# One program from the output projection to the end of the first expert pass, with the table of tokens made by one-hot products

## The chip, the cores and the metric

The kernel runs on one core of a Trainium2 chip. The metric is device time in microseconds (us) of one execution. Three executions of the kernel before took 1960.2, 1954.55 and 1946.48 us, a median of 1954.55. The profiled execution is a further one. All data are float32.

The engines are named as in the profile: PE (TensorE, matmuls; its weight loads are PEld), DVE (VectorE), ACT (ScalarE), POOL (GpSimd) and SP (SyncE, which here only issues DMAs).

## The reference

One layer of a hybrid decoder over 1024 prompt tokens and 64 sample tokens: T = 1088 tokens, D = 1024. The change touches what follows the RWKV and attention heads:

```python
h = h + concatenate([rw_out, rmsnorm(att)]) @ w_out            # output projection, 1024x1024
x = rmsnorm(h, norm_ffn)                                       # router: 4 group + 32 expert logits
gsel = argmax(x @ rgw + rgb)                                   # one of 4 groups
top_p, top_i = top_k(softmax(le_sel), 2)                       # two of the group's 8 experts
wts = pg_sel * top_p / sum(top_p)
y = sum over the two experts e of wts_e * ((silu(x @ wg_e) * (x @ wu_e)) @ wd_e)   # 1024->256->1024
h = h + y
h = h + sigmoid(rmsnorm(h) @ ple_gate_w) * (p @ ple_proj)
y_out = rmsnorm_final(h)
```

## The kernel before

The kernel is a row of programs. Each is a block in which the five engines run their own instruction streams and meet at the end. Ahead of each, `g.clear` makes a small block in which POOL clears that program's semaphores one by one. The order is: `project_tokens`, `lora_inputs`, `rwkv`, `attention`, then the part that matters here, `out_projection`, `route` (two blocks), `experts`, and last `finish`. Tokens are handled in TT = 9 tiles of 128 rows, of which the last has 64.

**rwkv to attention.** `rwkv`'s SP stream ends with a wait for all its projections and then issues the load of attention's first weights (`g.w3`, 1.5 MB, line 389). Attention's first matmul (L1227) waits for it.

**out_projection** (from L1537). PE first makes nine column sums for the norm of the attention half (L1600). Then each tile takes 32 matmul passes of 512 columns: 16 for the RWKV half (L1623), 16 for the attention half (L1628), into four PSUM banks; odd tiles use the other four. DVE adds the halves to `g.h` (L1588, L1592) and ACT sums the squares (L1561). PE does nothing else in this block.

**route, first block** (from L1633). SP loads ten constants (gain of the norm, router weights, masks). DVE waits for all ten, then makes the normed rows `xn` tile by tile (L1693); SP stores them to DRAM (`g.xn`); PE turns each tile (8 transposes, L1707), ACT copies it out of PSUM, PE makes the logits (16 passes of 96 columns, L1720), DVE adds the bias (L1682). SP loads the inputs of the embedding product last, and the block ends when they have landed.

**route, second block.** DVE chooses the experts with a serial chain of small operations, each followed by a drain (L1760 to L1788), then PE counts the tokens ahead of each (`rank`, L1858 to L1860), and DVE works out for both choices k the slot of every token in a table and its row in the output (L1801 to L1824, about 36 operations for each k). POOL then writes the token numbers into the DRAM table with 18 indirect DMAs (L1879, one for each k and tile) and waits for them. Beside it PE makes the embedding product `p @ ple_proj` (L1867), and SP loads the weights of experts 0, 1 and 2.

**experts** (from L1895). After the clear come a block that sets `now`, the load of the largest count into a register, and a block that clears semaphores again. `one_pass` then loads the table into `idx` (L1936), gathers 128 rows for each of 32 experts with indirect DMAs from POOL (L1948), and runs a pipeline over the experts: turn (8 transposes, L1958), DVE copy (L2026), up (64 passes of 128 columns, L1972), silu on ACT (L2014), product on DVE (L2035), down (8 passes of 512 columns, L1982), copy and store by ACT (L2000, L2003). PE's order is up(e), turn(e+1), down(e-1). SP loads expert e into one of four slots once down(e-4) is done. A last block gathers the results (18 indirect DMAs, L2071) and adds them into `g.h` (L2052). Later passes, for experts with more than 128 tokens, stand behind a branch; with these inputs the branch isn't taken.

**finish** (from L2079) loads the gate weights, turns the normed rows, multiplies and stores the output.

Of the kernel before, what the change touches and what calls it, by code (L numbers as in the profile page):

```python
# [6 lines left out]
D = 1024  # L7
KD = D // 128
S = 1024
# [209 lines left out]
def rwkv(nc, g):  # L219

    with ExitStack() as ctx:
# [107 lines left out]
        with nc.Block() as block:  # L329
            @block.sync  # L330
            def _(sp):
# [33 lines left out]
                for j in range(-1, J + 1):  # L365
# [1164 lines left out]
WR = 96  # L1530

# [5 lines left out]
def out_projection(nc, g):  # L1537

    with ExitStack() as ctx:
        sb = lambda n, s: ctx.enter_context(nc.sbuf_tensor(n, s, f32))  # L1540
        sem = g.semaphores(nc, ctx)
        bank = g.bank
        wo = g.wo
        junk = sb("ojunk", [128, D])
        rstd = sb("orstd", [128, TT])
        summed, meaned, rooted, gained, projected, added, zeroed = (
            sem("o_" + n) for n in "summed meaned rooted gained projected added zeroed".split())
        g.clear(nc)
        with nc.Block() as block:
            @block.gpsimd  # L1550
            def _(pool):
                pool.memset(g.h[64:128, TT - 1, :], 0.0).then_inc(zeroed, 1)

            @block.scalar
            def _(act):
                act.wait_ge(meaned, 1)
                act.activation(rstd[:, :], rstd[:, :], ACT.Sqrt).then_inc(rooted, 1)
                act.wait_ge(zeroed, 1)
                for t in range(TT):
                    act.wait_ge(added, t + 1)  # L1560
                    act.activation(junk[:, :], g.h[:, t, :], ACT.Square, accum_out=g.ss[:, t:t + 1])  # L1561
                    act.drain()

            @block.vector
            def _(dve):
                c = PC["attn_norm"]
                for j in range(J):
                    dve.wait_ge(g.wo_in[J + j], 16)
                    dve.tensor_scalar(wo[:, J + j, :], wo[:, J + j, :], g.prm[:, c + j:c + j + 1], None, ALU.mult).then_inc(gained, 1)
# [806 lines left out]
```

## Time and profile before

| what | value |
|---|---|
| median of three executions | 1954.55 us |
| profiled execution | 1968.97 us, span 1967.0 us |
| PE busy | 1672.5 us (85%) |
| DVE, ACT, POOL busy | 657.9, 430.0, 70.3 us |
| mean granted TensorE clock | 0.899 |
| DMA | 247.01 MB, mean 126 GB/s |

The page's slices of the span, each a fortieth (49 us):

```profile
PE   3687997998998888898989889966599999990897
PEclk8888898898898658899999989988699999995899
DMA  3033031221000004424242530044399999956211
```

Each digit is a tenth: the share of the slice in which the engine was busy, the clock granted to TensorE, and the busy share of the DMA engines. The programs touched run from about 1158 us (slice 24) to 1821 us (slice 37). The row of PE dips at slices 26 to 28, is 9 through the expert pipeline, and is 0 where the results are gathered.

### The profile page before, as it was taken

To read this page: it belongs to the slowest core of one execution; us is meant where nothing else is said; L and a number is where in the kernel's file an instruction comes from. 1 tells how busy PE (TensorE), PEld (TensorE's weight loads), DVE (VectorE), ACT (ScalarE), POOL (GpSimd) and SP (SyncE) were. 2 spreads that over 40 slices of the span, in tenths; PEclk is the share of its full clock that TensorE was granted. 3 is DMA by queue.
4 is the path that set the end of the run, shared out by engine and by line. 5 is a ranking of instruction groups with operands and counts; after the bars stand their busy time and mean duration, and the time that the engine had idled before them with its cause. 6 is when DMAs were issued, how large, how long until landed. Compare 5 with 4: busy or idle time off the path is not lost. (4 is left out here: it accounts for less than half of the span.)

```text
span 1967.0 us, 34999 instructions
## 1 busy us (share of the span) xinstructions
PE 1672.5 (85%) x15260; PEld 1173.9 (60%) x15260; DVE 657.9 (33%) x1559; ACT 430.0 (22%) x856; POOL 70.3 (4%) x76
## 2 busy tenths in 40 slices
PE   3687997998998888898989889966599999990897
PEld 2355666576577666575766654452488888870443
DVE  3125455445455231514251532235011111114333
ACT  2131321321321210413132320022011111112233
POOL 0000000000000000000000000003100000004000
PEclk8888898898898658899999989988699999995899
DMA  3033031221000004424242530044399999956211
GB/s 119 12 58 24 5 21 15 34 15 21 16 2 9 13 21 188 162 108 162 108 162 108 222 132 0 0 165 193 128 357 364 362 374 364 370 205 214 108 43 38
DMA packets 61774, 247.01 MB, mean 126 GB/s; under 512 B 13745, under 2 KB 21169, under 8 KB 51889
## 3 DMA queue, kind: packets, MB, share of 16 engines
q1 hardware_dynamic: 49232, 201.70, 30.8%
q0 software_dynamic: 7776, 26.23, 3.6%
q10 hardware_dynamic: 4608, 16.78, 2.1%
q8 instruction: 123, 2.02, 0.5%
q14 instruction: 35, 0.28, 0.0%
HBM read 210.65 MB, written 34.04 MB: 124 GB/s over the span
## 5 line engine op out<-in xcount | busy, mean ns | idle before, releaser
L415 PE MATMUL bank<-h,w 128*128 128x352 f32 (+1 forms) x576 | 200.7, 499 | 6.4 <-DVE xb L978 6.4
L415 PEld LDWEIGHTS bank<-h,w 128*128 128x128 f32 x576 | 110.5, 199 | 70.6 <-issue 8.7
L2026 DVE COPY xgT<-bank 128x512 f32<-128x512 f32 x64 | 41.2, 686 | 319.2 <-PE bank L1958 319.2
L1972 PEld LDWEIGHTS bank<-xgT,we_g 128*128 128x128 f32 x1024 | 122.0, 196 | 17.7 <-issue 14.3
L1227 PE MATMUL bank<-h,w 128*128 128x352 f32 (+1 forms) x384 | 120.7, 477 | 9.7 <-DMA w<-in_wqkv 9.7
L1972 PE MATMUL bank<-xgT,we_g 128*128 128x128 f32 x1024 | 122.5, 279 | 2.8 <-DVE xgT L2026 2.8
L1972 PE MATMUL bank<-xgT,we_u 128*128 128x128 f32 x1024 | 119.6, 275 | 0.0
L1972 PEld LDWEIGHTS bank<-xgT,we_u 128*128 128x128 f32 x1024 | 116.9, 192 | 0.0
L1982 PE MATMUL bank<-we_d,hT 128*128 128x512 f32 x256 | 115.0, 592 | 0.0
L2169 PE MATMUL bank<-wp,unT 128*128 128x512 f32 x256 | 113.3, 601 | 0.0
L1227 PEld LDWEIGHTS bank<-h,w 128*128 128x128 f32 x384 | 74.1, 194 | 54.6 <-POOL qd L1213 10.3
L2169 PEld LDWEIGHTS bank<-wp,unT 128*128 128x128 f32 x256 | 48.9, 193 | 58.8 <-issue 58.8
L1982 PEld LDWEIGHTS bank<-we_d,hT 128*128 128x128 f32 x256 | 46.3, 191 | 46.4 <-issue 46.4
L1283 PE MATMUL bank<-ident,score 128*128 128x128 f32 x288 | 46.3, 295 | 27.2 <-ACT score L1402 14.1
L1243 PEld LDWEIGHTS bank<-w,h 128*128 128x128 f32 (+1 forms) x576 | 65.3, 186 | 2.6
L1958 PE MATMUL bank<-ident,xg 128*128 128x128 f32 x256 | 34.7, 280 | 37.4 <-DMA xg<-xn_rows,idx 37.4
L1243 PE MATMUL bank<-w,h 128*128 128x128 f32 (+1 forms) x576 | 66.0, 275 | 0.0
L1283 PEld LDWEIGHTS bank<-ident,score 128*128 128x128 f32 x288 | 32.6, 147 | 51.4 <-ACT score L1402 27.8
L2000 ACT ACTIVATE yo<-bank 128x512 f32<-128x512 f32 x64 | 34.7, 594 | 123.7 <-PE bank L1982 123.7
L1430 DVE TENSOR_TENSOR eT<-bank,sin 128x352 f32<-128x352 f32 (+1 forms) x24 | 12.8, 535 | 142.3 <-PE bank L1235 140.8
L1466 DVE CUSTOM_DVE_ANT_0 score<-bank,count 128x512 f32<-128x512 f32 (+3 forms) x96 | 50.8, 555 | 27.5 <-PE bank L1272 27.5
L1623 PE MATMUL bank<-cache,rwT 128*128 128x512 f32 x128 | 59.4, 618 | 0.0
(399 smaller groups left out, 2579.0 us busy)
## 6 DMA issues: line engine op xcount, KB each, us to landing
we_g<-in_weg SPq DMA_DIRECT2D x32, 1024.0 KB, 7.2
we_u<-in_weu SPq DMA_DIRECT2D x32, 1024.0 KB, 9.9
we_d<-in_wed SPq DMA_DIRECT2D x32, 1024.0 KB, 12.7
cache<-in_kcj SPq DMA_DIRECT2D x4, 5120.0 KB, 16.0
cache<-in_vcj SPq DMA_DIRECT2D x4, 5120.0 KB, 15.0
y_rows<-yo ACTq DMA_DIRECT2D x32, 512.0 KB
w<-in_wrkv SPq DMA_DIRECT2D x12, 512.0 KB, 11.5
w<-in_wqkv SPq DMA_DIRECT2D x4, 1536.0 KB, 18.2
```

Of the source, the lines that this page charges most:

```text
L415: mm = pe.matmul(out[:, 0:w], w3[:, KIND[q], kd, :], g.uT[:, kd, a:a + w], start=(kd == 0), stop=(kd == KD - 1))
L1227: mm = pe.matmul(bank[QK[i][n]][:, 0:w], w3[:, k, i, :], g.uT[:, k, a:a + w], start=(k == 0), stop=(k == KD - 1))
L1243: mm = pe.matmul(bank[2 + n % 2][0:rows, 128 * (t - t0):128 * (t - t0) + 128], g.uT[:, k, 128 * t:128 * t + rows], w3[:, k, 2, :], start=( ...
L1283: mm = pe.transpose(bank[x % 2][:, 128 * (b - b0):128 * (b - b0) + 128], score[:, i % 2, hh, 128 * b:128 * b + 128], g.ident[:, :])
L1466: dve.tensor_tensor_reduce(out=score[:, i % 2, hh, 512 * b:512 * b + w], in0=bank[4 + 2 * hh + (b if i >= 4 else i % 2)][:, 0:w], in1=coun ...
L1623: pe.matmul(bank[b + i][:, :], g.rwT[:, k, 128 * t:128 * t + 128], wo[:, k, 512 * i:512 * i + 512], start=(k == 0), stop=(k == J - 1))
L1958: mm = pe.transpose(bank[k // 4][:, 128 * (k % 4):128 * (k % 4) + 128], v[:, k, :], g.ident[:, :])
L1972: mm = pe.matmul(bank[2 + e % 2][:, 128 * (2 * a + f):128 * (2 * a + f) + CAP], w[:, k, 128 * f:128 * f + 128], xT[e % 2][:, k, :], start= ...
L1982: mm = pe.matmul(bank[4 + 2 * (e % 2) + c][:, :], hT[e % 2][:, f, :], weights[e % NW][2][:, f, 512 * c:512 * c + 512], start=(f == 0), sto ...
L2000: last = act.activation(yo[:, e % 2, 512 * c:512 * c + 512], bank[4 + 2 * (e % 2) + c][:, :], ACT.Copy)
L2026: last = dve.tensor_copy(xT[e % 2][:, 4 * c:4 * c + 4, :].rearrange("p k q -> p (k q)"), bank[c][:, :])
L2169: mm = pe.matmul(bank[4 + 2 * (t % 2) + i][:, :], uT[:, t % 2, k, :], wp[:, k, 512 * i:512 * i + 512], start=(k == 0), stop=(k == KD - 1))
```

## The change

Five things, all in the programs named above.

1. `out_projection`, both blocks of `route` and the first pass of `experts` are one block, `feed_forward`, with one clear of 46 semaphores ahead of it. Buffers share memory by time: norm gain and router weights lie in expert slot 1, embedding inputs and masks in slot 3, `xn` and the gather buffers in attention's `g.w3`, and slot 2 in the cache tensor whose front held `w_out`.
2. PE's order is written out: project(t), turn(t-1), logit(t-2); then embedding tiles between the last turns and logits, between the choice of experts, `rank` and `find`. Each projection bank is its own semaphore count (`evicted`), and the projection uses banks 0 to 3 alone. PE waits for all eleven constants ahead of the first project(t).
3. The table isn't written to DRAM. DVE makes `place[k]` (token x position in the expert, 1 where it fits) and `tokens[k]` (one-hot of the expert times the token number), and PE multiplies them: `idx[position, expert]` = sum over tokens. Slot and row numbers (`rows(k)`) are worked out on DVE in the pipeline, at experts 1 and 2.
4. `combine` (the results of the first pass) has a clear of 6 semaphores of its own. `later_passes` has a clear of 19 and makes the DRAM table itself, behind the branch.
5. `rwkv` issues the load of attention's first weights once the last projections are made, inside the SP loop.

```diff
@@ rwkv, SP @@
                         if jn + 2 < J:
                             load_small(jn + 2)
-
-                for q in "rkv":
-                    sp.wait_ge(s[q + "_mm"], 3 * J)
-                sp.dma_start(g.w3[:, :], g.d_wqkv[0].rearrange("p k i c -> p (k i c)")).then_inc(g.qkv_in, 16)
+                    if jn == J - 1:
+
+                        for q in "rkv":
+                            sp.wait_ge(s[q + "_mm"], 3 * J)
+                        sp.dma_start(g.w3[:, :], g.d_wqkv[0].rearrange("p k i c -> p (k i c)")).then_inc(g.qkv_in, 16)
@@ feed_forward, SP @@
+                for dst, src in LOADS:
+                    if dst is i32t:
+                        sp.wait_ge(s["summed"], 1)
+                    sp.dma_start(dst, src).then_inc(s["consts"], 16)
+                sp.dma_start(pp, g.d_pproj.rearrange("(k p) n -> p k n", p=128)).then_inc(s["p_in"], 16)
+                sp.dma_start(pT, g.d_pT.rearrange("(k p) n -> p k n", p=128)).then_inc(s["p_in"], 16)
+                load_expert(sp, g, weights[0], 0, w_in[0])
                 for t in range(TT):
...
+                sp.wait_ge(s["projected"], 4 * TT)
+                load_expert(sp, g, weights[2], 2, w_in[2])
+                sp.wait_ge(s["logits"], TT)
+                load_expert(sp, g, weights[1], 1, w_in[1])
+                sp.wait_ge(s["p_done"], TT)
+                sp.wait_ge(s["idx"], 1)
+                load_expert(sp, g, weights[3], 3, w_in[3])
+                for e in range(NW, NE):
+                    sp.wait_ge(s["down"], e - NW + 1)
+                    load_expert(sp, g, weights[e % NW], e, w_in[e % NW])
@@ feed_forward, POOL @@
+                for i in range(3):
+                    pool.wait_ge(kept[i], 16 * len(range(i, TT, 3)))
+                pool.wait_ge(s["idx"], 1)
+                for e in range(NE):
+                    if e >= NX:
+                        pool.wait_ge(s["x_turned"], e - NX + 1)
+                    pool.indirect_dma_start(xg[e % NX], None, g.xn[:, :], bass.IndirectOffsetOnAxis(idx[:, e:e + 1], 0)).then_inc(xg_in[e % NX], 16)
@@ feed_forward, PE @@
+                def find():
+
+                    for k in range(2):
+                        pe.wait_ge(s["placed"], k + 1)
+                        for t in range(TT):
+                            mm = pe.matmul(bank[7][:, 0:NE], place[k][:, t, :], tokens[k][:, t, :], start=(k == 0 and t == 0), stop=(k == 1 and t == TT - 1))
+                    mm.then_inc(s["found"], 1)
...
+                mm.then_inc(s["summed"], 1)
+                pe.wait_ge(s["consts"], 16 * len(LOADS))
+                for t in range(TT):
+                    project(t)
+                    if t >= 1:
+                        turn(t - 1)
+                    if t == 2:
+                        pe.wait_ge(s["meaned"], 1)
+                    if t >= 2:
+                        logit(t - 2)
+                pe.wait_ge(s["p_in"], 32)
+                embed(0)
+                embed(1)
+                turn(TT - 1)
+                logit(TT - 2)
+                embed(2)
+                logit(TT - 1)
+                embed(3)
+                embed(4)
+                embed(5)
+                rank()
+                embed(6)
+                find()
+                embed(7)
+                embed(8)
+                gather_turn(0)
@@ feed_forward, DVE, per tile @@
+                def normed(t):
+                    x = ffn[:, t:t + 1]
+                    dve.wait_ge(s["squared"], t + 1)
+                    dve.tensor_scalar(x, g.ss[:, t:t + 1], 1.0 / D, RMS_EPS, ALU.mult, ALU.add).then_inc(s["f_meaned"], 1)
+                    dve.wait_ge(s["f_rooted"], t + 1)
+                    dve.reciprocal(x, x)
@@ feed_forward, DVE, the choice @@
+                    op(dve.tensor_tensor(oh[k][:, :, :], oh[k][:, :, :], bt(valid[:, :], NE), ALU.mult))
...
+                dve.tensor_tensor(tokens[0], oh[0][:, :, :], bt(tokv[:, :], NE), ALU.mult)
+                dve.wait_ge(s["ranked"], 1)
+                dve.tensor_tensor(tokens[1], oh[1][:, :, :], bt(tokv[:, :], NE), ALU.mult)
+                for k in range(2):
+                    op(dve.tensor_tensor(v32[:, :, :], oh[k][:, :, :], bank[4][:, 0:TT * NE].rearrange("p (t e) -> p t e", t=TT), ALU.mult))
+                    op(dve.tensor_reduce(position[:, k, :], v32[:, :, :], AX.X, ALU.add))
+                    dve.tensor_tensor(place[k], bc(iota, 128), bt(position[:, k, :], 128), ALU.is_equal).then_inc(s["placed"], 1)
+                op(dve.tensor_reduce(most, bank[5][:, 0:NE], AX.X, ALU.max))
+                dve.tensor_copy(g.most[:, :], most)
+                dve.wait_ge(s["found"], 1)
+                dve.tensor_copy(idx[:, :], bank[7][:, 0:NE]).then_inc(s["idx"], 1)
...
+                gates()
+                gather_out(0)
+                for e in range(NE):
...
+                    if e in (1, 2):
+                        rows(e - 1)
```

`gates()` holds the seven small operations that made the weights of the two experts ahead of `rank` before.

## Rows read from the trace of the kernel before

**Rows 1.** Windows of the expert pipeline: us, busy and count of each engine, clock, DMA.

```profile
core 0: us, PE busy (x) PEld busy (x) DVE busy (x) ACT busy (x) POOL busy (x), PEclk, DMA share, GB/s
1412.00:1773.00 361.00, 359.06 (x2486) 297.30 (x2484) 50.49 (x94) 46.20 (x96) 26.29 (x28) 1.00 0.89 331
```

**Rows 2.** Timeline from rwkv to attention: start us, us, engine, instruction, [idle before <-releaser].

```profile
741.36 0.20 POOL L1211 MEMSET vt<- 64x128 f32 x1 [740.90 <-POOLq L2297]
743.02 4.44 PE L1227 MATMUL bank<-h,w 128*128 128x352 f32 x7 [9.69 <-DMA w<-in_wqkv]
```

**Rows 3.** Timeline of the output projection, PE and the last DVE operation ahead of it.

```profile
1156.15 1.29 DVE L1423 TENSOR_TENSOR sqsum<-sqsum,dscore 128x1088 f32<-128x1088 f32 x1 [1.17 <-ACT dscore L1417]
1158.56 3.85 PE L1600 MATMUL bank<-ones,sqsum 128*128 128x1 f32 x18 [3.93 <-PEq L2297]
1162.34 10.15 PE L1623 MATMUL bank<-cache,rwT 128*128 128x512 f32 x16
...
1179.19 7.03 PE L1623 MATMUL bank<-cache,rwT 128*128 128x512 f32 x16
...
1261.59 7.03 PE L1623 MATMUL bank<-cache,rwT 128*128 128x512 f32 x16
```

**Rows 4.** Timeline of the router's first block.

```profile
1288.54 0.34 POOL L1676 MEMSET zeros<- 128x290 int32 x1 [129.08 <-POOLq L2297]
...
1294.98 3.67 DVE L1693 SCALAR_TENSOR_TENSOR xn<-h,rrstd,ffn_gain 128x1024 f32<-128x1024 f32 x3 [5.58 <-DMA tok<-in_tok]
...
1302.40 1.04 PE L1707 MATMUL bank<-ident,xn 128*128 128x128 f32 x8
...
1305.03 1.04 PE L1707 MATMUL bank<-ident,xn 128*128 128x128 f32 x8
```

**Rows 5.** Timeline of the choice of experts.

```profile
1327.55 0.19 DVE L1760 TENSOR_REDUCE mx<-lg 128x9 f32<-128x36 f32 x1 [4.54 <-PEq L2297]
...
1337.00 0.46 DVE L1784 TENSOR_TENSOR cnt<-cnt,valid 128x288 f32<-128x288 f32 x1
...
1340.27 0.75 PE L1858 MATMUL bank<-cnt,upper 128*128 128x288 f32 x2
...
1341.48 10.97 PE L1867 MATMUL bank<-pp,ppT 128*128 128x512 f32 x25
```

**Rows 6.** Timeline of attention and windows behind it: PE after a gap of 3.5 us.

```profile
1110.49 0.86 PE L1283 MATMUL bank<-ident,score 128*128 128x128 f32 x2 [3.53 <-ACT score L1402]
```

**Rows 7.** Window of attention, just after that gap (columns as in Rows 1).

```profile
1112.00:1114.00 2.00, 2.00 (x10) 0.80 (x8) 0.94 (x4) 0.67 (x4) 0.00 (x0) 0.50 0.95 410
```

**Rows 8.** Timeline from the scatters to the first expert.

```profile
1386.04 0.06 DVE L1921 MEMSET now<- 128x1 f32 x1 [22.75 <-PEq L2297]
1388.26 0.34 SPq L1936 DMA_DIRECT2D idx<-table  x1
...
1390.22 0.97 POOL L1948 DMA_INDIRECT xg<-xn_rows,idx  x1 [15.04 <-DMA idx<-table]
...
1398.14 1.97 PE L1958 MATMUL bank<-ident,xg 128*128 128x128 f32 x8 [37.37 <-DMA xg<-xn_rows,idx]
...
1401.49 6.63 PE L1972 MATMUL bank<-xgT,we_g 128*128 128x128 f32 x32 [1.38 <-DVE xgT L2026]
```

**Rows 9.** Timeline of the expert pipeline: DVE's copy, and PE at experts 25 apart.

```profile
1448.49 3.73 PE L1972 MATMUL bank<-xgT,we_g 128*128 128x128 f32 x32
...
1456.72 1.29 DVE L2026 COPY xgT<-bank 128x512 f32<-128x512 f32 x2 [9.86 <-PE bank L1958]
...
1735.32 3.73 PE L1972 MATMUL bank<-xgT,we_g 128*128 128x128 f32 x32
```

**Rows 10.** Timeline of the gather of the results.

```profile
1777.80 0.94 POOL L2071 DMA_INDIRECT xg<-y_rows,row_i  x1 [56.01 <-DVE row_i L2047]
...
1782.39 1.28 DVE L2052 SCALAR_TENSOR_TENSOR h<-xg,weight,h 128x1024 f32<-128x1024 f32 x1 [4.81 <-DMA xg<-y_rows,row_i]
...
1789.42 1.92 POOL L2071 DMA_INDIRECT yo<-y_rows,row_i  x1 [0.81 <-DVE h L2052]
```

More of the change, by code:

```diff
@@ L1635, in route, with feed_forward @@
+def feed_forward(nc, g):
     with ExitStack() as ctx:
@@ new lines, in feed_forward @@
+        m2 = g.spare[:, 420:420 + 2 * TT].rearrange("p (k t) -> p k t", k=2)
+        most = g.spare[:, 440:441]
+        oh = [sb(f"oh{k}", [128, TT, NE]) for k in range(2)]
+        v32 = sb("v32", [128, TT, NE])
+        i32t = g.spare[:, 444:444 + NE]
+        valid, tokv = sb("valid", [128, TT]), sb("tokv", [128, TT])
+        pad_a, position = sb("pad_a", [128, 2, TT]), sb("position", [128, 2, TT])
+        idx = g.idx = sb("idx", [128, NE], i32)
+        ple_p = g.ple_p
+        names = ("summed meaned rooted gained projected evicted added zeroed squared f_meaned f_rooted consts xnorm turned evac logits lev "
+                 "p_in shifted exped counted ranked placed found idx p_done p_out "
+                 "x_turned xev up silu h down yev stored0 stored1").split()
@@ L1745, in route, with embed_out @@
-        pg, dl = sb("pg", [128, TT]), sb("dl", [128, TT])
-        eg = sb("eg", [128, TT, G])
-        g.clear(nc)
-        with nc.Block() as block:
+                def embed_out(t):
+                    r = rows_of(t)
+                    act.wait_ge(s["p_done"], t + 1)
+                    for i in range(2):
+                        b = 2 * (t % 2)
+                        made = bank[b + i][:, :] if t < TT - 1 else bank[b][TS * i:TS * i + TS, :]
+                        last = act.activation(ple_p[0:r, t, 512 * i:512 * i + 512], made, ACT.Copy)
+                    last.then_inc(s["p_out"], 1)
@@ new lines, in _ @@
+                c = PC["attn_norm"]
+                for j in range(J):
+                    dve.wait_ge(g.wo_in[J + j], 16)
+                    dve.tensor_scalar(wo[:, J + j, :], wo[:, J + j, :], g.prm[:, c + j:c + j + 1], None, ALU.mult).then_inc(s["gained"], 1)
+                dve.wait_ge(s["summed"], 1)
+                dve.memset(rstd, 1.0)
+                dve.memset(most, 0.0)
+                dve.drain()
+                dve.tensor_scalar(rstd[:, 0:8], bank[7][:, 128:136], 1.0 / RW, RMS_EPS, ALU.mult, ALU.add)
@@ L1824, in _ @@
-                    dve.tensor_copy(g.turn[:, k, :], over[:, :]).then_inc(placed, 1)
-                    dve.drain()
-                op(dve.tensor_reduce(most[:, :], bank[1][:, 0:NE], AX.X, ALU.max))
-                dve.tensor_copy(g.most[:, :], most[:, :])
-            @block.sync
-            def _(sp):
-                for e, slot in enumerate(g.weights):
-                    load_expert(sp, g, slot, e, w_in)
-                sp.wait_ge(w_in, 48 * len(g.weights))
+                    op(dve.tensor_scalar(t1, p, float(n), None, ALU.mult))
@@ L1895, in experts, with later_passes @@
-def experts(nc, g):
-    NW, NX = 4, 3
-    AHEAD = len(g.weights)
+                pool.wait_ge(rows, 1)
+                for n in range(2 * TT):
+                    t, k = n // 2, n % 2
+                    if n >= 4:
+                        pool.wait_ge(combined, n - 3)
+                    pool.indirect_dma_start(y[n % 4][:, :], None, g.yb[:, :], bass.IndirectOffsetOnAxis(row[:, k, t:t + 1], 0)).then_inc(y_in[n % 4], 16)
+def later_passes(nc, g):
     with ExitStack() as ctx:
@@ L1935, in _ @@
                 def _(sp):
[L1936 to L1940 removed]
+                    sp.dma_start(tok[:, :], g.d_tok).then_inc(s["tok_in"], 16)
+                    sp.dma_start(g.table[:, :], g.d_zeros).then_inc(s["zero_in"], 16)
```

762 lines of the change are left out of this document (394 added, 368 removed).

## The prediction

> **What bounds the kernel now.** I read the waits of PE first, then the windows by stage, then the timeline across every border of the programs touched. PE is the bound wherever it has work: through the expert pipeline it is busy 359.06 of 361 us at the full clock [rows 1], and in the output projection it runs tile after tile with no gap [rows 3]. So time can come only from the stretches in which PE waits. The largest ends at the first expert: PE sits idle 37.37 us [rows 8], while DVE works out slots, POOL scatters token numbers, two clears and a register load pass, and the table is read back. Smaller ones lie at each border: from the last projection to the first turn at 1296 us, from the last logit to the second router block, and 9.69 us ahead of attention [rows 2]. After each gap PE also restarts at half clock (1.2 GHz, granted 0.50) and pays again. The reader should see in the rows which program border each gap crosses; the sum below replays the new order with the durations of the old one.
>
> **The change part by part**, as absolute times of the profiled execution.
>
> *The start of the block.* The clear of 7 semaphores with its barriers took 1158.5 - 1157.4 = 1.1 us (POOL and ACT start with PE's row; DVE's last operation ends at 1157.44) [rows 3]. The new clear has 46. A clear of 16 together with a register load took 1388.26 - 1386.04 = 2.2 us [rows 8], so one more semaphore costs at most (2.2 - 1.1)/9 = 0.13 us, and at least nothing: 0 to 5 us more. I take 0.08 each, since that row holds the register load too: 39 x 0.08 = 3.1, and the block begins at 1161.6. PE then waits for all constants ahead of project(0). Ten took 1294.98 - 1288.54 = 6.4 us [rows 4]; the eleventh adds an SP issue of about 0.5. SP's own wait, for PE's column sums, costs nothing: they take 3.85 us [rows 3] and ten issues take longer. PE starts projecting at 1161.6 + 6.9 = 1168.5 instead of 1162.34: **6.2 us lost**. Queued behind that wait is everything else on PE. DVE's gains on `w_out` are done by then.
>
> *Projection with the router woven in.* The first tile took 1179.19 - 1162.34 = 16.85 us, 3.1 more than a warm one, since PE came from a gap [rows 3]; PE comes from a gap now too, so I keep it: 1185.4. A warm tile is (1261.59 - 1179.19)/6 = 13.73 us [rows 3]; seven make 96.1, the last, of half as many passes, 6.9. Woven in are eight turns and seven logits; a pair takes 1305.03 - 1302.40 = 2.63 us and a lone turn 1.04 [rows 4]: 7 x 2.63 + 1.04 = 19.5. PE reaches the first embedding tile at 1307.9. Nothing holds PE in between: a bank is evicted during the tile that filled it, and the norm of tile t (about 5 us of DVE and ACT in turn) has the 13.7 us of project(t+1) to hide under. If that cover went, each tile would pay the excess; that is a rival below. Embedding tiles are 8 passes of 10.97/25 = 0.43 us [rows 5] = 3.43. Two, a turn with its logit, a third and the last logit are 6.9 + 2.6 + 3.4 + 1.8 = 14.7: the last logit at 1322.6, DVE begins to choose at about 1323.0. Before it began at 1327.55 [rows 5], so it is **4.5 us ahead**: the weaving repays the 6.2 lost, and the two borders are gone.
>
> *Choice and rank.* The chain keeps its operations, drops one of 288 columns and adds two (0.46 us [rows 5], about 0.53 with the drain, an estimate): `counted` at 1340.27 - 4.5 + 0.5 = 1336.3. PE has embedding tiles 3 to 5 until 1322.6 + 10.3 = 1332.9 and then a gap of 3.4 us. In attention a gap of 3.53 us [rows 6] was followed by a clock of 0.50 [rows 7]; the gap here is the nearest to it, so I take half clock for the next 5 us. `rank` took 1341.48 - 1340.27 = 1.2 us warm [rows 5], 2.4 now: ranked at 1338.8. Embedding tile 6 takes 5.0 instead of 3.4: 1343.8.
>
> *The table.* DVE: one product, then for each k a product, a reduce (0.53 each) and the comparison `place` over 128x1152. That form isn't in the trace; the sum over 128x1088 took 1.29 us [rows 3], so 1.29 x 1152/1088 = 1.37. Placed at 1341.8 and 1344.3. PE: `find` is 36 passes of 32 columns on 128x128 weights. Bounds: 0.12 us a pass, as turn and logit with 24 passes in 2.63 [rows 4] (0.11), and 0.21, as the column sums of 18 passes in 3.85 at half clock [rows 3]: 4.0 to 7.6 us. Warm is nearest: 4.3, from 1343.8 to 1348.1, `idx` at 1348.5. None of the 18 scatters, the slot arithmetic ahead of them, their landing, the clear, or the read of the table is left ahead of it.
>
> *The first gather.* From issue to use 4.6 us in the gather of the results, where no load of weights is in flight [rows 10], and 7.9 us before the first expert, where three were [rows 8]. Experts 0 to 2 have landed by then and expert 3 is issued later, so 4.6: 1353.2. PE makes embedding tiles 7 and 8 meanwhile (5.2 us, to 1353.3). First turn at 1353.3 instead of 1398.14: **44.8 us gained**. DVE's seven `gates` operations run beside this gather. The longest issue on POOL beside DVE's two-input operations took 1.92 us instead of 0.94 [rows 10], so this could add 1.0 us. The Trainium skill, "SBUF — State Buffer", section "SBUF: two separate sides", has a rule against the change here: DVE with two SBUF inputs and POOL lock a shared port against each other for a whole instruction, and descriptor writing can starve. By that rule the gather would start only behind `gates`, some 1.8 us later, and the sum would be 45 instead of 47; the row allows half of it, and no run so far shows a small operation doing it.
>
> *Warm start of the experts.* Before, the first turn took 1.97 us against 1.04 [rows 8, 4] and the first 32 passes 6.63 against 3.73 [rows 8, 9]: 3.8 us. With PE in work until then **3.8 us are gained**. If the clock still is down, nothing.
>
> *The pipeline.* (1735.32 - 1448.49)/25 = 11.47 us an expert [rows 9], bound by PE, with the same instructions after. `rows(0)` and `rows(1)`, about 33 small operations (0.19 us for one of that kind [rows 5], 0.25 with its drain, an estimate) or some 8.5 us each, lie in DVE's gaps; the gap ahead of its copy is 9.86 us [rows 9]. Zero; if they overran, two copies would be late by a microsecond and PE would wait, 2 us at most.
>
> *Behind it.* The clear of 6 for `combine` is new: 1.1 us, as that of 7, **1.0 lost**. `later_passes` clears 19 and loads the register on the way to `finish`: 1.1 + 12 x 0.08 + about 0.5 for the load = **2.5 lost** (2.2 to 4).
>
> *Attention's weights.* They land early, and PE can start when the block does: 743.02 - 741.4 = **1.6 us gained** [rows 2]; the rest of the 9.69 us is the clear. SP's new wait ahead of the last stores finds its projections done.
>
> **Sum**: 44.8 + 3.8 + 1.6 - 1.0 - 2.5 = 46.7, say 47 us. Against the profiled execution's own 1968.97 that is 1922. It ran 14.4 us above the median of the three, with no row that says why; against the median, 1954.55 - 47 = **1907.5 us**.
>
> **Bounds.** Low: clears 2 + 3.5 more (0.13 each), `find` +3.3, gather +3.3, `gates` +1.8, no warm start -3.8 leaves about 30. High: no half clock at `rank` +3 and clears at nothing +4: 54. With the three runs' spread of 5 to 8 us around their median: 1895 to 1926.
>
> **Rivals.** (a) *A small gain, 20 to 35 us*: the new serial chain (constants, rank, find, gather) each meets its upper bound, PE has gaps there and enters the experts at half clock. For it: a gap of 3.5 us is enough [rows 6, 7], and PE has three waits in a row there. Against it: embedding tiles fill two of them. Time 1927. (b) *No change*: the per-tile chain isn't hidden. DVE and ACT would have to need more than 13.73 + 2.63 = 16.4 us a tile, by 47/9 = 5.2, so 21.6 us; the chain is two adds, two multiply-adds, square, root, reciprocal and norm, about 7 us. Also here: the table comes out as late as before, because `find` waits for both k. Time 1955. (c) *Slower, by the loads in the expert pipeline.* The DMA share there is already 0.89 [rows 1] in the mean. If slot 2, now in the cache tensor, or the gathers made an expert's transfers slow enough to hold PE, all 32 periods would stretch. It decides from 47/32 = 1.5 us a period, 13.0 instead of 11.47; at 13.7 the time is 1954.55 - 47 + 32 x 2.2 = 1978. Against it: PE has no wait for weights there, bytes and slots are the same, and expert 3 is issued some 30 us ahead of its use. (d) *A larger gain, over 54 us*: borders cost more than the rows of PE show. Time 1898.
>
> **How the numbers follow.** Forecast (gain 40 to 54) 0.68, (a) 0.15, (b) 0.05, (c) 0.04, (d) 0.08. 1% is 19.5 us, about what a measurement of this kernel can tell from no change. Faster: 0.68 + 0.15 + 0.08 = 0.91. Same 0.05, slower 0.04. The range 1895 to 1926 holds the forecast, most of (d) and the better half of (a).
>
> **What would show it.** In the changed kernel's trace: PE's first projection pass about 7 us behind its column sums' start; tiles of 16.4 us; DVE's choice some 160 us after the first projection; 36 small passes ending about 25 us after the choice began; no scatter; the first turn of an expert about 30 us after the choice began, at granted 1.00; a period of 11.47; 6 to 8 us between the last sum of `combine` and `finish`. A wait of PE ahead of project(t) would make me wrong by (b), one for weights by (c).

## The result: 48 us less, and where they came from

The changed kernel took 1905.6 us (median of four executions, 1899.4 to 1908.0) beside 1954.1 for the kernel before: a ratio of 0.9753, 95% interval 0.973 to 0.978. In later rounds on another chip it took 1905.5 beside 1952.6. The prediction was 1907.5. Two executions in a slow state are left out of all medians: one of the kernel before (1976.6 us, granted clock 0.88) and one of a kernel below (2562 us, 0.63).

Its profiled execution has a span of 1897.6 us. That is 69.4 less than the 1967.0 of before, and the first thing to learn is which part of that to believe. The last store of the rows ahead of attention comes at 718.77 us, against 734.94 (the kernel before, then the changed one):

```profile
734.94 0.33 SPq L378 DMA_DIRECT2D rw_rows<-xb  x1
718.77 0.33 SPq L378 DMA_DIRECT2D rw_rows<-xb  x1
```

Nothing of the code up to there changed but one load, so 16.2 us of the difference were there before the change was reached; the first two experiments below show that the load isn't their cause. What is left is 53.2, of which 3.9 lie in stretches whose instructions are the same. The touched stretches give 49.3, and the medians differ by 48.4.

**Stages**, each the time between two landmarks of the timelines, in us ("last copy" is the start of ACT's last copy of results; "last sum" in the last row is ACT's last sum of squares in the combining):

| from, to | before | predicted | after |
|---|---|---|---|
| last store of rows, attention's first matmul | 8.08 | 6.5 | 6.78 |
| last sum of squares in attention, first projection | 4.90 | 11.1 | 10.52 |
| first projection, start of the choice | 165.2 | 154.5 | 153.7 |
| start of the choice, first turn of an expert | 70.6 | 30.3 | 29.1 |
| first turn, last copy of results | 374.3 | 370.5 | 370.5 |
| last copy, combining | 4.21 | 5.2 | 4.92 |
| combining | 40.1 | 40.1 | 39.4 |
| last sum, finish | 4.2 | 6.7 | 6.6 |

The waits of PE show the same at a glance. First the kernel before, from the start of the output projection on (engine, line, what it waited for, us, times, longest):

```profile
PE bank L1958 <- DMA xg<-xn_rows,idx: 37.4, 1, 37.4
PE bank L1707 <- DVE xn L1693: 13.8, 1, 13.8
PE bank L1867 <- PEq L2297: 4.8, 1, 4.8
PE bank L1600 <- PEq L2297: 3.9, 1, 3.9
PE bank L1972 <- DVE xgT L2026: 2.8, 2, 1.4
```

And the changed kernel, the same stretch:

```profile
PE bank L1755 <- PEq L2430: 7.0, 1, 7.0
PE bank L1737 <- DVE cache L2000: 2.8, 2, 1.4
PE bank L1668 <- DMA mixed<-in_i32t: 2.5, 1, 2.5
PE bank L1706 <- DVE gated L1947: 2.5, 1, 2.5
PE bank L1724 <- DMA w<-xn_rows,idx: 0.7, 1, 0.7
```

Three waits of 56 us together have gone; in their place stand a longer clear (7.0 instead of 3.9), the last of the constants (2.5), the counts (2.5) and a rest of 0.7 at the gather. The 2.8 us ahead of the first two experts are in both.

The start of the new block, in its timeline (start, us, engine, instruction, [idle before <- releaser]), which answers to [rows 3]:

```profile
1142.32 3.85 PE L1755 MATMUL bank<-ones,mixed 128*128 128x1 f32 x18 [6.99 <-PEq L2430]
1142.32 3.44 DVE L1900 TENSOR_SCALAR cache<-cache,prm 128x1024 f32<-128x1024 f32 x4 [4.17 <-PEq L2430]
1146.91 0.43 SPq L1613 DMA_DIRECT2D mixed<-in_i32t  x1
1148.66 2.08 PE L1668 MATMUL bank<-cache,mixed 128*128 128x512 f32 x2 [2.49 <-DMA mixed<-in_i32t]
```

And the chain from the choice to the first expert, which answers to [rows 5, 8]:

```profile
1302.37 0.19 DVE L1923 TENSOR_REDUCE mixed<-mixed 128x9 f32<-128x36 f32 x1
1314.85 0.75 PE L1706 MATMUL bank<-gated,we 128*128 128x288 f32 x2 [2.48 <-DVE gated L1947]
1316.07 5.38 PE L1697 MATMUL bank<-we 128*128 128x512 f32 x8
1317.69 1.36 DVE L1955 TENSOR_TENSOR cache<-we,position 128x1152 f32<-128x1152 f32 x1
1320.01 1.36 DVE L1955 TENSOR_TENSOR cache<-we,position 128x1152 f32<-128x1152 f32 x1
1321.28 4.10 PE L1715 MATMUL bank<-gated,cache 128*128 128x32 f32 x36
1325.42 0.19 DVE L1959 CAST idx<-bank 128x32 int32<-128x32 f32 x1 [3.71 <-PE bank L1715]
1326.50 1.08 POOL L1640 DMA_INDIRECT w<-xn_rows,idx  x1 [183.28 <-DVE idx L1959]
1331.50 1.16 PE L1724 MATMUL bank<-ident,w 128*128 128x128 f32 x8 [0.74 <-DMA w<-xn_rows,idx]
1334.03 7.41 PE L1737 MATMUL bank<-cache,we 128*128 128x128 f32 x64 [1.38 <-DVE cache L2000]
```

Read it downward: DVE counts, PE ranks, DVE compares twice, PE looks the tokens up in 36 small passes, DVE casts, POOL gathers. PE waits 2.48 us ahead of the ranks and then makes them at the full clock (1.2 us); the granted clock falls only behind them, and tile 6 of the embedding, which fills the time of the comparisons, takes 5.38 us instead of 3.6. The windows across it (us, PE busy and count, granted clock, DMA share, GB/s):

```profile
1314.00:1316.00 2.00, 1.15 (x6) 1.00 0.00 0
1316.00:1318.00 2.00, 2.00 (x6) 0.58 0.00 0
1318.00:1320.00 2.00, 2.00 (x4) 0.57 0.00 0
1320.00:1322.00 2.00, 2.00 (x12) 1.00 0.00 0
```

The 0.57 and 0.58 are means: in windows of 1 us the clock is 0.66, 0.50, 0.50 and 0.64 from 1316 to 1320, so PE had the lower of its two levels (0.50, 1.2 GHz) for a little over 3 us.

The first expert then starts at full clock, 7.41 us for 64 passes. The pipeline is what it was [rows 1], 358.62 of 360 us busy:

```profile
1340.00:1700.00 360.00, 358.62 (x2497) 1.00 0.89 334
```

### The profile page after: what moved, and what is told of

It reads as the page before. It is cut to its first block and busy times, and to the rows that moved or that the text cites. A ratio compares the mean times of both kernels' runs of the same rounds, so it can differ in the third digit from the quotient of the medians.

```text
span 1897.6 us, 35039 instructions
## 1 busy us (share of the span) xinstructions
PE 1644.1 (87%) x15296; PEld 1154.2 (61%) x15296; DVE 665.5 (35%) x1589; ACT 430.3 (23%) x864; POOL 52.4 (3%) x57
## 5 line engine op out<-in xcount | busy, mean ns | idle before, releaser
L1737 PEld LDWEIGHTS bank<-cache,we 128*128 128x128 f32 x1536 | 175.1, 192 | 13.7 <-issue 10.5
L1737 PE MATMUL bank<-cache,we 128*128 128x128 f32 x1536 | 175.6, 275 | 2.8 <-DVE cache L2000 2.8
L2000 DVE COPY cache<-bank 128x512 f32<-128x512 f32 x64 | 41.2, 686 | 291.7 <-PE bank L1724 291.7
L1668 PE MATMUL bank<-cache,mixed 128*128 128x512 f32 x256 | 113.1, 601 | 2.5 <-DMA mixed<-in_i32t 2.5
L1749 PE MATMUL bank<-we,gated 128*128 128x512 f32 x192 | 86.4, 592 | 0.0
L1668 PEld LDWEIGHTS bank<-cache,mixed 128*128 128x128 f32 x256 | 48.9, 193 | 61.5 <-issue 59.0
L1814 ACT ACTIVATE cache<-bank 128x512 f32<-128x512 f32 x64 | 34.7, 594 | 123.6 <-PE bank L1749 123.6
L1737 PEld LDWEIGHTS bank<-cache 128*128 128x128 f32 x512 | 58.4, 192 | 3.8 <-issue 3.8
L2286 PE MATMUL bank<-ident,un 128*128 128x128 f32 x72 | 11.2, 307 | 55.7 <-DVE un L2246 55.7
L1737 PE MATMUL bank<-cache 128*128 128x128 f32 x512 | 58.5, 275 | 0.0
```

The costliest lines, as they stand in the source:

```text
L1668: mm = pe.matmul(bank[2 * part + i][:, :], rows[:, k, 128 * t:128 * t + 128], wo[:, J * part + k, 512 * i:512 * i + 512], start=(k == 0), ...
L1737: mm = pe.matmul(bank[6 + e % 2][:, 128 * (2 * a + f):128 * (2 * a + f) + CAP], w[:, k, 128 * f:128 * f + 128], xT[e % 2][:, k, :], start= ...
L1749: mm = pe.matmul(bank[2 * (e % 2) + c][:, :], hT[e % 2][:, f, :], weights[e % NW][2][:, f, 512 * c:512 * c + 512], start=(f == 0), stop=(f ...
L1814: last = act.activation(yo[:, e % 2, 512 * c:512 * c + 512], bank[2 * (e % 2) + c][:, :], ACT.Copy)
L2000: last = dve.tensor_copy(xT[e % 2][:, 4 * c:4 * c + 4, :].rearrange("p k q -> p (k q)"), bank[4 + c][:, :])
L2286: mm = pe.transpose(bank[2 * (t % 2) + k // 4][:, 128 * (k % 4):128 * (k % 4) + 128], un[:, t % 2, 128 * k:128 * k + 128], g.ident[:, :])
```

## The experiments

The theory is that of the prediction: PE is the bound, so the gain is the sum of the waits that end sooner: above all the table's path and the program borders inside it. The rivals in the experiments divide that gain otherwise.

**One load alone.**

```diff
 # rwkv, SP, in the kernel before
-        for q in "rkv": sp.wait_ge(s[q + "_mm"], 3 * J)     # behind the stores
-        sp.dma_start(g.w3[:, :], ...)
+        if jn == J - 1:                                     # ahead of the last stores
+            for q in "rkv": sp.wait_ge(s[q + "_mm"], 3 * J)
+            sp.dma_start(g.w3[:, :], ...)
```

> The kernel before with one part of the change alone: the load of attention's first query, key and value weights is issued while the last head block of the previous program runs, not at its end. Theory (the sum): PE's first attention matmul comes 1.3 us sooner behind the last store of the rows (6.8 us instead of 8.08), nothing else moves, and the time stays within what can be measured (ratio 0.997 to 1.001). Rival: in the one profiled run of the changed kernel the stages ahead of attention were 16 us shorter than in the one of the kernel before; if the early load had caused that, this kernel would be about 16 us faster (ratio 0.992) and reach the last store of the rows at about 719 us of its profile instead of 735.

Measured: 1954.1 us beside 1955.0, ratio 1.0005 (0.998 to 1.003). From the last store to attention's first matmul it took 6.78 us. The last store came at 727.94, between the two profiles. The next experiment doesn't have the early load and has its last store at 719.22, as soon as the changed kernel's. So the 16 us are spread between executions, as far as single profiles can show it: a profile's span alone would have credited the change with them.

**The table without the merging.**

```diff
 # route, second block, of the kernel before
-    dve.tensor_copy(g.turn[:, k, :], over[:, :]).then_inc(placed, 1)
+    dve.tensor_tensor(place[k], iota == pos).then_inc(placed, 1)    # behind pos
 # PE, ahead of its last embedding tile
+    for k in range(2): for tt in range(TT): pe.matmul(bank[1][:, 128:160], place[k][:, tt, :], tokens[k][:, tt, :])
-    POOL: 18 indirect DMAs into g.table, and the wait for them
 # experts, pass 0
-    sp.dma_start(idx[:, :], g.table ...)
```

> The kernel before, its programs kept apart, with the table alone made by one-hot products and left in SBUF for the expert program; the table that later passes would read isn't written (they don't run on these inputs). Theory: the router's second block ends with DVE's arithmetic at about 1367.5 us of the profile instead of with the landed scatters at 1386.0, and 2 us of reading the table back are gone: 16 to 21 us faster than the kernel before, about 1936, ratio 0.990 to 0.992; the rest of the change's 48 us then needs the one program. Rival: the table is nearly the whole gain, 38 us or more (ratio 0.981 or less), and the merging gives little.

Measured: 1935.9 us, ratio 0.992 (0.989 to 0.995), as the theory had it. The stretch from the choice to the first turn is 55.1 us instead of 70.6, 15.5 less. The timeline of that kernel shows what the borders do with a list that is ready:

```profile
1348.71 0.18 DVE L1835 CAST g_idx<-bank 128x32 int32<-128x32 f32 x1
1358.14 1.08 POOL L1955 DMA_INDIRECT xg<-xn_rows,g_idx  x1 [85.56 <-POOLq L1932]
1366.71 1.97 PE L1965 MATMUL bank<-ident,xg 128*128 128x128 f32 x8 [14.98 <-DMA xg<-xn_rows,g_idx]
```

The list lies there at 1348.9, and POOL may use it only at 1358.14: PE still has its last tile, and then come two clears and the register load. The gather itself takes 8.6 us instead of 5.0, with an expert's weights issued beside it, and PE starts cold.

**The merging without the table.**

```diff
 # feed_forward, in the changed kernel
-    place[k], tokens[k], find(), idx from bank 7
+    DVE: gates behind rows(0), rows(1), each with then_inc(s["placed"], 1)
+    POOL: for k: wait placed; 9 indirect DMAs tok -> g.table
+    SP: wait for the 18; sp.dma_start(idx[:, :], g.table ...)
```

> The changed kernel, one program, but its table of tokens per expert is made as before: DVE works out all slots, POOL scatters 18 columns of token numbers into the table in DRAM, and the first expert's list is read back from it. Theory: the table's path is what PE waits for. From the ranks on: 8.5 us of slot arithmetic, 18 scatters at 1.27, 10.7 us until they have landed, 2 of reading back and 4.6 of gather put the first turn of an expert about 63 us behind the start of the choice (29.1 in the changed kernel, 70.6 in the one before), and PE restarts cold for 3.8 more: 36 us slower than the changed kernel (32 to 40), about 1942 us, ratio to the kernel before 0.994. Rival: the borders between the programs are what cost, and the scatters are as well hidden beside the embedding tiles: not over 10 us slower than the changed kernel, about 1915, ratio 0.980.

(The clear has 48 semaphores here, and a load that zeroes the table is added.) Measured: 1941.2 us, ratio 0.995 (0.993 to 0.997), 35.6 above the changed kernel in its own rounds; the theory had 36. Its timeline, POOL and SP from the first scatter to the first expert:

```profile
1331.21 1.14 POOL L1643 DMA_INDIRECT table<-tok_i,slot_a  x1 [184.18 <-DVE turn L1992]
...
1352.90 0.96 POOL L1643 DMA_INDIRECT table<-tok_i,slot_a  x1 [0.30 <-issue]
1360.03 0.33 SPq L1628 DMA_DIRECT2D idx<-table  x1
1363.21 0.97 POOL L1648 DMA_INDIRECT w<-xn_rows,idx  x1 [9.35 <-DMA idx<-table]
1371.06 1.97 PE L1732 MATMUL bank<-ident,w 128*128 128x128 f32 x8 [41.59 <-DMA w<-xn_rows,idx]
```

22.7 us of issuing, 6.2 until the last scatter has landed, 3.2 for reading 32 numbers a partition back, 7.9 for the gather beside a load: 64.3 us from the choice to the first turn. Embedding tiles can't cover it, since PE has only three left. **Each half alone is worth little: 19 us for the table (1955.0 - 1935.9), 10.5 for the merging (1951.8 - 1941.2, the medians of its own rounds), and 48 together.** The traces, from attention's last sum to the end, have 17.2, 8.8 and 50.1. The other 19 us are there only when a list made on chip can be used in the same program at once.

**Is it the weaving?**

```diff
 # PE in feed_forward (ACT and DVE follow)
     for t in range(TT):
         project(t)
-        if t >= 1: turn(t - 1)
-        if t >= 2: logit(t - 2)
     embed(0); embed(1)
+    for t in range(TT): turn(t); logit(t - 1)
```

> The changed kernel, but PE projects all nine tiles first and only then turns the normed tiles and makes the logits (ACT and DVE follow: all evictions and squares first, then the norms). PE's work is the same. Theory: the weaving is what hides the norm of a tile; with three buffers of normed rows, six of the nine norms (some 4 to 5 us of DVE and ACT in turn) come behind the projections, where PE has 2.63 us of work a tile: the choice starts 10 to 20 us later than in the changed kernel (first projection to choice 164 to 174 us instead of 153.7), time about 1920. Rival: the gain there comes from the borders taken away and not from the weaving: at most 4 us slower than the changed kernel, about 1908.

Measured: 1909.5 us, ratio 0.979 (0.976 to 0.982); the changed kernel had 1905.6. From the first projection to the choice 158.3 us, 4.6 more than woven and 6.9 less than before. The rival was right, and the theory's 10 to 20 us were not there. PE and DVE in that stretch:

```profile
1271.67 7.11 PE L1697 MATMUL bank<-we 128*128 128x512 f32 x16 [1.72 <-DVE h L1880]
1281.60 1.09 PE L1677 MATMUL bank<-ident,w 128*128 128x128 f32 x8 [1.95 <-DVE w L1896]
1282.12 1.28 DVE L1896 SCALAR_TENSOR_TENSOR w<-h,mixed,we 128x1024 f32<-128x1024 f32 x1
1285.32 1.28 DVE L1896 SCALAR_TENSOR_TENSOR w<-h,mixed,we 128x1024 f32<-128x1024 f32 x1
```

A norm comes every 2.3 to 3.2 us, not every 4 to 5: squares had been summed beside the projections, and the steps of neighbouring tiles overlap. PE has 2.63 us of turn and logit for each. It waits twice, 3.7 us in all, and only one of the two waits is for a norm: the first, 1.72, is for DVE's last evictions ahead of the embedding tiles. The second, 1.95, is for the norm that DVE began at 1280.26; its root on ACT stood behind the copies of the embedding tiles, and DVE waited 5.35 us for it. The 13.8 us wait in the kernel before, at its first turn, came from the border: constants loaded only then, and the first norm behind them.

**The wait for the constants, and the clears.**

```diff
 # constants later: PE
-    pe.wait_ge(s["consts"], 16 * len(LOADS))
     for t in range(TT):
         project(t)
+        if t == 1: pe.wait_ge(s["consts"], 16 * len(LOADS))
 # cleared ahead: attention, POOL
     pool.memset(qd[:, :, :, :], 0.0).then_inc(s["zeroed"], 1)
+    for semaphore in g.ahead: pool.sem_clear(semaphore)       # all 93 of the later programs
 # feed_forward, combine, later_passes, finish
-    g.clear(nc)
+                                                               # semaphores from g.taken
```

> The changed kernel, but PE waits for the constants only behind its second projected tile (the first instruction of PE that reads one is the first logit, two tiles later). Theory: the 2.5 us that PE waited ahead of its first projection pass, for the last of eleven constants, were a wait for nothing that it needed: they go, and the whole is 2.5 us faster than the changed kernel, about 1903 (ratio to the kernel before 0.974). Rival: PE then waits as long for something else that arrives at the same time (the output weights or the gains), or the projection runs ahead of DVE's evictions: no difference.

> The changed kernel, but the 109 semaphores of the four programs behind attention are allotted ahead of attention and cleared in POOL's stream there, where POOL has no other work; the four clearing blocks (46, 6, 19 and 22 semaphores plus the barrier of each) go. Theory: a border costs 0.078 us a semaphore and about 0.26 for a barrier, on every engine: 3.9 us at the start of the output projection, 0.7 at the combining and 3.7 at the finish are gained, 8.3 in all, about 1897 us, ratio to the kernel before 0.971. The POOL work of 8.5 us in attention costs nothing. Rival: the engines wait at these borders for their instruction streams or for transfers, not for the clears: under 3 us gained, 1903 or more.

> Both edits of the last two together: PE waits for the constants behind its second tile, and the semaphores of the programs behind attention are cleared inside attention. Theory: the two gains add, 8.3 + 2.5 = 10.8 us against the changed kernel, about 1895 us, ratio to the kernel before 0.970. Rival: they overlap, and the sum is no more than the larger of the two.

The expectation's 109 is a miscount: its own four numbers, and the list in the kernel, make 93.

Measured: constants later 1903.5 us (ratio 0.977, 0.974 to 0.980), cleared ahead 1897.8 (0.974, 0.970 to 0.977), both 1893.9 (0.971, 0.968 to 0.975). The differences to the changed kernel are too small for these intervals, so the traces must say. With the constants later PE starts 2.6 us sooner, as expected, 1.1 of it is given back by the start of the choice, and 0.8 comes back by the first turn. With the semaphores cleared ahead, the finish starts 1.5 us behind the last sum instead of 6.6, more than the 3.7 expected, and the combining 0.7 sooner; but the output projection starts no sooner at all, 11.1 us behind attention's last sum instead of 10.5. Its timeline:

```profile
1143.35 3.71 PE L1764 MATMUL bank<-ones,mixed 128*128 128x1 f32 x18 [3.19 <-PEq L1180]
1146.07 0.75 DVE L1909 TENSOR_SCALAR cache<-cache,prm 128x1024 f32<-128x1024 f32 x1 [3.10 <-DMA cache<-in_wout]
1149.94 0.75 DVE L1909 TENSOR_SCALAR cache<-cache,prm 128x1024 f32<-128x1024 f32 x1 [0.55 <-DMA cache<-in_wout]
1154.04 2.93 PE L1677 MATMUL bank<-cache,mixed 128*128 128x512 f32 x3 [6.98 <-DMA mixed<-in_i32t]
```

The block's first matmul comes 3.8 us sooner behind attention (0.4 instead of 4.2), but now the last rows of `w_out` are still landing, DVE's gains wait for them one by one, and the constants, issued behind, land as late as before: PE's wait grows from 2.5 to 7.0 us. The DMA windows show the two loads side by side: in this kernel the share is 1.0 (about 410 GB/s) from 1138 to 1149 us, while in the changed kernel it falls to 0.33 as the block starts at 1142; the last constant is used 5.3 us behind its issue instead of 1.75. The clear had been cover for a load. Both edits together take PE's wait away: it starts projecting 4.1 us behind attention instead of 10.5, the 6.4 us that the theory expects there (3.9 + 2.5). But the constants later alone give 2.6 there and the clears ahead alone -0.6: the clear's share is to be had only when PE doesn't wait for the constants. From attention's last sum to the end the traces have 759.5 us in the changed kernel, 758.1, 755.0 and 748.0, so 1.4, 4.5 and 11.5 less. The kernel cleared ahead met the 1897 expected by its median alone; its trace has little over half of the 8.3. Read on one chip, with the changed kernel as control:

> The changed kernel itself, on the same chip and in the same rounds as the kernels that build on it, so that differences under 1% are read side by side. Every theory expects what was measured: ratio to the kernel before 0.973 to 0.978.

> The kernel with both edits (semaphores of the later programs cleared inside attention, PE's wait for the constants two tiles later), beside the changed kernel on the same chip. Theory: 8 to 12 us below the changed kernel's median there (ratio between the two 0.994 to 0.996). Rival: what the earlier run showed was the spread between runs, and the two lie within 3 us.

Measured: the changed kernel 1905.5 us (ratio to before 0.977, 0.975 to 0.979), both edits 1891.1 (0.969, 0.967 to 0.971). The slowest of five executions with both, 1892.8, is below the fastest without, 1898.9. The medians are 14.4 us apart, more than the 8 to 12 expected; from attention's last sum to the end the traces differ by 11.8 (748.2 us instead of 760.0).

**One embedding tile in another place.**

```diff
     embed(5)
-    rank()
     embed(6)
+    rank()
     find()
```

> The changed kernel with one line of PE's order changed: embedding tile 6 comes ahead of the ranks, not behind them. PE's 2.5 us wait for the counts is then filled, but nothing lies between the ranks and the look-up of the tokens, where DVE works 3.3 to 5.5 us on the positions and the first comparison. Theory of the clock (a gap of some 2.5 to 3.5 us costs half the clock for the next microseconds, as behind the ranks in the changed kernel): tile 6 takes 3.4 instead of 5.4 us, but the 36 look-up passes then follow the gap and take 5 to 7.6 us instead of 4.1; the first turn of an expert comes 1 to 3 us later than 29.1 us behind the start of the choice. Rival (the gap costs nothing but itself): the look-up is done as soon as DVE's second comparison is, some 0.9 us sooner, and the first turn comes at 28.2. The whole time can't tell these; the trace can.

Measured: 1909.4 us, ratio 0.978 (0.974 to 0.982). The first turn comes 33.5 us behind the start of the choice instead of 29.1, 4.4 later: the theory of the clock was right in sign, and its 1 to 3 us were too few. The timeline and a window:

```profile
1328.18 7.89 PE L1715 MATMUL bank<-gated,cache 128*128 128x32 f32 x36 [2.88 <-DVE cache L1955]
1335.88 6.57 PE L1697 MATMUL bank<-we 128*128 128x512 f32 x8
```

```profile
1329.00:1341.00 12.00, 12.00 (x40) 0.50 0.16 49
```

A wait of 2.5 us became one of 2.9, and PE then ran at 0.50 (1.2 GHz) from 1328 to about 1341 us, some 13 us, where in the changed kernel it was a little over 3. The look-up takes 7.9 us instead of 4.1 and tile 7 6.6 instead of 3.7; the first turn follows tile 8 with no wait, so PE's slow work is what delays it.

That the wait alone lowers the clock isn't shown, and other runs speak against it. Seven kernels, the changed one among them, have the same wait of 2.5 us ahead of the ranks, and in each the clock falls just behind the ranks and tile 6 takes 5.2 to 5.4 us. But with the constants later it stays at 1.00 for 9 us behind that wait and falls behind the look-up (tile 6 takes 3.68 us and tile 7 5.38). In the merged kernel with scatters, which has no look-up, it doesn't fall while PE works. And in the kernel before with the table on chip no wait of PE over 0.7 us lies in the 29 us ahead, and the clock falls in the middle of the look-up. In this order (constants later, twice; merged with scatters; table on chip, twice):

```profile
1317.00:1326.00 9.00, 8.98 (x51) 1.00 0.00 0
1327.00:1329.00 2.00, 2.00 (x4) 0.50 0.17 29
1319.00:1329.00 10.00, 9.72 (x30) 1.00 0.00 1
1343.00:1346.00 3.00, 3.00 (x27) 1.00 0.00 0
1347.00:1351.00 4.00, 4.00 (x14) 0.50 0.00 0
```

So the 36 passes of 32 columns, which keep PE busy by its row, can be followed by the lower clock as a wait can. Here the two stand side by side, and the slow stretch is the longest; which of them it is due to, one trace can't tell.

**A wider combining.** On the kernel with both edits:

```diff
-        y = [sb(f"yk{i}", [128, D]) for i in range(4)]
+        y = [sb(f"yk{i}", [128, D]) for i in range(8)]
-                    if n >= 4: pool.wait_ge(combined, n - 3)
+                    if n >= 8: pool.wait_ge(combined, n - 7)
```

> Both edits of before, and in the combining of the experts' results eight row buffers instead of four, so that a gather waits for the sum eight back. Theory: in the changed kernel 18 gathers and sums took 39.4 us, in most of which a gather was issued only when a sum four back was done and landed 4 us later (four gathers in flight per 4 to 5 us of latency and 1.6 of waiting); with eight, POOL's issues of 1.25 us or DVE's sums of 1.4 us set the pace: 5 + 18 x 1.4 = 30 us, so 5 to 9 us less than the kernel with both edits, about 1887. Rival: DVE's sums and POOL's gathers hold each other up (an issue took 1.92 us beside a sum), and the pace stays at 2 us a row: under 2 us gained.

Measured: 1889.0 us, ratio 0.968 (0.965 to 0.971), the fastest kernel of the study, 2.1 us or 0.1% below the one with both edits, which the intervals don't separate. The windows of the combining, four buffers and then eight (us; busy and count of PE, PEld, DVE, ACT, POOL; clock, DMA share, GB/s):

```profile
1694.85:1734.73 39.88, 0.00 (x0) 0.00 (x0) 23.73 (x23) 10.34 (x18) 20.37 (x18) 0.50 0.72 237
```

```profile
1699.92:1734.49 34.57, 0.00 (x0) 0.00 (x0) 23.78 (x23) 10.34 (x18) 21.10 (x18) 0.50 0.76 273
```

5.3 us less in the trace, at the low end of what was expected. The first sum begins 5.5 us behind the start (5 expected), the 18 sums take 27.9 us, 1.55 each instead of 1.4, and ACT's last square, which the 30 us had left out, adds 1.2. Twelve of POOL's last fourteen issues took 1.05 to 1.91 us, beside DVE's sums, instead of 0.94; in the second half DVE's sums follow each other almost without a gap.

## Why the prediction was right

**The start of the block** was costed at 6.2 us lost, measured 5.6. The clear of 46 semaphores took 4.18 us where that of 7 took 1.12: 0.078 us each, as taken. PE's wait for the constants began its projection 6.3 us behind the column sums, for 6.9 taken. The phrase that DVE's gains are done by then holds only with this clear ahead of them: the clear and the load of `w_out` run beside each other, and with the clear gone its 3.8 us came back only with the other wait gone too.

**Projection and router**: 10.7 predicted from the first projection to the choice, 11.5 measured; PE's row has 153.71 busy of 153.71 us, and a tile takes 16.4 us, as forecast. The sum was right and a phrase of it wrong. It said that the weaving repays the start; unwoven the gain is still 6.9 of 11.5. The borders repaid most of it, and rival (b), which needed 21.6 us a tile, was further off than thought: even 2.6 us of cover a tile nearly suffices.

**Choice to first turn**: 40.3 predicted, 41.5 measured. The gap ahead of the ranks was 2.5 us instead of 3.4. The ranks took 1.2 us at the full clock, where 2.4 at half were taken; the clock fell behind them, for a little over 3 us instead of 5, and tile 6 took 5.4 (5.0 taken). `place` took 1.36 (1.37), the look-up 4.1 (4.3, between bounds of 4.0 and 7.6). The bounds were real: with the order changed by one line the same 36 passes took 7.9. The list was ready 23.2 us behind the start of the choice, 2.3 sooner than forecast, and 1.1 of that was given back between the list and the first turn, so the sum of this stretch is nearer than its parts. That the gap would be followed by half clock was taken from one row of attention; the runs above show that it need not be.

**The gather** took 5.0 us from issue to use, 4.6 taken, and its issue began 0.9 us behind the cast of the list, which stood in no term. DVE's seven `gates` operations ran beside that, from 1325.52 to 1327.26. The first issue took 1.08 us and the next 0.93, so 0.15 us were paid. The Trainium skill ("SBUF — State Buffer", section "SBUF: two separate sides") has POOL blocked for the whole of each DVE operation with two SBUF inputs, and it says so only for POOL operations that read SBUF. Only three of the seven are of that kind, 0.17 us each, all inside the first issue: 0.5 us at most, and not the 1.8 of the prediction, which counted all seven. The 0.15 measured is less than either. For long operations the runs agree in sign: in the combining, issues took up to 1.9 us beside sums of 1.28, against 0.94 alone; that POOL stood for a whole sum isn't shown, since with eight buffers, where the sums of the second half follow each other, five of seven issues took 1.07 or 1.08.

**Warm start and pipeline**: 3.8 predicted and measured; the period is the same. `rows(0)` runs on DVE from 1353.58 to 1361.43 and its next copy starts at 1363.51, released by PE: hidden with 2 us to spare. Rival (c) had nothing: no wait for weights stands in PE's list above.

**The borders behind** cost 0.7 and 2.4 us, 1.0 and 2.5 taken. **Attention's weights** gave 1.3 of 1.6.

Together 49.3 us in the touched stretches for 46.7 predicted, and 48.4 in the medians. Rival (a) needed every serial step at its upper bound, and none came there: a semaphore cost 0.078 us (bound 0.13), the look-up 4.1 (7.6), the gather 5.0 (7.9). The 14.4 us by which the profiled execution of before lay above its median were set aside as unexplained. The other profiles, with the same code up to there, reach the last store ahead of attention 7 to 24 us sooner, so they most likely lay in those stages; no run repeats that execution. Two slips in the working had no effect: the 3.5 us more for the later clears in the low bound are not worked out in it (18 semaphores at 0.05 more are 0.9), and the range adds the runs' spread at its lower end (1900.5 - 5) but hardly at its upper one (1924.6 + 1).

## What to carry to other kernels

Look at what a serial chain ends in: making a small table on chip gained 19 us and merging the programs 10.5, but both together 48, because the list is of use only to a program that is already running. Price a border by its semaphores and by what it hides: take one away and look which transfer is late next. Before moving work into a gap of PE, see what it leaves next to the gap: the same 36 passes took 4.1 or 7.9 us by the place of one tile.

## What was not expected of the hardware

Clearing a semaphore costs 0.078 us on POOL, with every engine waiting; 93 of them cleared beside attention's work cost nothing that a trace shows (attention took 412.5 us with them and 412.6 without). Two clearing blocks with 41 semaphores were 5.1 us of the way to the finish. The granted clock fell to 0.50 for a little over 3 us just behind the ranks in seven traces with a PE wait of 2.5 us ahead of them, 9 us behind the same wait in an eighth, and not at all in a ninth; in a tenth it fell inside the look-up, with no such wait ahead. With a wait of 2.88 us right ahead of the look-up it lasted some 13 us. Code that is the same in every kernel but for one load reached the same landmark, the last store ahead of attention, anywhere between 711 and 735 us of a profile, so two profiles are compared by stretches between landmarks and not by their ends.
